# A sixth set of expert weights in a hybrid streaming encoder step on one core

## The reference, cut to what matters

```python
proj = jnp.einsum('blnc,ncd->blnd', branches, w_out)                  # 2 branches x 512 -> 1024
x = x + jnp.sum(gates * proj.astype(jnp.float32), axis=2).astype(x.dtype)
h2 = rmsnorm(x, norm_ffn_g)
x = x + hier_moe(h2, w_router_group, b_router_group, w_router_expert, b_router_expert,
                 w_expert_gate, w_expert_up, w_expert_down)
# in hier_moe, for a block of rows of expert e:
return (jax.nn.silu(xblk @ w_gate[e]) * (xblk @ w_up[e])) @ w_down[e]
```

## Time and profile before

| | |
|---|---|
| median of 3 runs | 1670.44 us (1666.98 to 1670.96) |
| the profiled execution | 1668.39 us |
| its span, first to last instruction | 1666.24 us (shown as 1666.2) |
| mean granted TensorE clock | 0.966 of full speed |
| TensorE busy | 1510.1 us, 91% of the span |
| `merge`, by its first and last instructions | 1113 to 1299 us |
| `experts` | 1300 to the end |

### The profile page before, as it was taken

How to read it: one execution, slowest core, us unless ns; L and a number is a source line. 1 busy time by engine, 2 the same in 40 slices (tenths; PEclk the granted TensorE clock), 3 DMA queues, 4 the chain that set the end, 5 groups by cost and what they waited for, 6 DMA issues and landing times. The chain is left out here.

```text
span 1666.2 us, 38766 instructions
## 1 busy us (share of the span) xinstructions
PE 1510.1 (91%) x16352; PEld 1070.4 (64%) x16352; DVE 861.3 (52%) x1874; ACT 445.3 (27%) x882; POOL 102.2 (6%) x102
## 2 busy tenths in 40 slices
PE   4999999969999999999998699978997799988894
PEld 2888888854566666666667466644554677766663
DVE  2454555455566676767668476645766233211111
ACT  2222222233222333233231244433453111111110
POOL 0000000000000000000000000000000222332321
PEclk9999999989999999999999699999999799999998
DMA  9332221535142232212122444436754699999972
GB/s 323 137 123 88 94 89 63 191 113 181 58 126 68 80 110 68 80 65 71 50 65 59 108 101 100 101 109 255 276 189 154 227 328 349 344 339 323 324 265 36
DMA packets 101326, 259.55 MB, mean 156 GB/s; under 512 B 34240, under 2 KB 53328, under 8 KB 91824
## 3 DMA queue, kind: packets, MB, share of 16 engines
q1 hardware_dynamic: 93424, 239.92, 42.3%
q0 software_dynamic: 7744, 17.33, 4.5%
HBM read 205.32 MB, written 60.56 MB: 160 GB/s over the span
## 5 line engine op out<-in xcount | busy, mean ns | idle before, releaser
L527 PEld LDWEIGHTS a_ps<-a_hT,a_wz 128*128 128x128 f32 x1792 | 202.6, 192 | 3.8 <-issue 3.8
L527 PE MATMUL a_ps<-a_hT,a_wz 128*128 128x128 f32 x1792 | 204.0, 275 | 0.0
L1918 PE MATMUL d_ps<-late,d_oT 128*128 128x512 f32 x256 | 115.4, 598 | 1.5 <-DVE d_oT L1687 0.8
L2089 DVE COPY f_xT<-f_turned 128x384 f32<-128x384 f32 x32 | 17.9, 558 | 164.9 <-PE f_turned L2056 164.9
L1918 PEld LDWEIGHTS d_ps<-late,d_oT 128*128 128x128 f32 x256 | 46.7, 190 | 51.5 <-issue 50.2
L1453 ACT ACTIVATE late<-c_score,c_top 128x1024 f32<-128x1024 f32 (+8 forms) x72 | 50.6, 703 | 93.2 <-DVE c_top L1402 92.6
L1101 PE MATMUL b_ps<-r_wg,r_hT 128*128 128x512 f32 x128 | 64.9, 640 | 11.5 <-POOL b_S L759 9.7
L2283 DVE TENSOR_SCALAR f_y<-f_down,table 96x512 f32<-96x512 f32 x32 | 23.9, 747 | 98.2 <-PE f_down L2082 98.2
L821 DVE TENSOR_TENSOR b_M<-b_ps,r_causal 128x512 f32<-128x512 f32 x72 | 46.4, 686 | 54.5 <-PE b_ps L1162 54.0
L2082 PE MATMUL f_down<-wd,f_midT 128*96 128x512 f32 x160 | 72.8, 598 | 1.8 <-DVE f_midT L2101 1.8
L2290 ACT ACTIVATE f_xT<-f_turned 128x384 f32<-128x384 f32 x32 | 15.7, 491 | 202.7 <-PE f_turned L2056 202.7
(11 more groups left out here) (363 smaller groups left out, 2847.5 us busy)
## 6 DMA issues: line engine op xcount, KB each, us to landing
wgu<-w_gate_up SPq DMA_DIRECT2D x20, 2048.0 KB
late<-w_gate_up SPq DMA_DIRECT2D x12, 2048.0 KB
wd<-w_down SPq DMA_DIRECT2D x20, 1024.0 KB
late<-w_down SPq DMA_DIRECT2D x12, 1024.0 KB
r_hT<-hT_d SPq DMA_DIRECT2D x18, 512.0 KB, 3.9
b_hT<-hT_d SPq DMA_DIRECT2D x18, 512.0 KB, 4.3
gate_d<-b_logits SPq DMA_DIRECT2D x32, 256.0 KB, 2.6
late<-gate_d SPq DMA_DIRECT2D x8, 1024.0 KB, 5.9
```

Source lines behind the costliest of these rows:

```text
L527: mm = pe.matmul(banks[Z_BANKS[n % 2]][:, j * P:(j + 1) * P], wz[:, i, (g + j) * P:(g + j + 1) * P], hT[t % 2][:, i, :], start=(i == 0), s ...
L1918: mm = pe.matmul(banks[2 + u][:], oT[t % 2][:, HB * branch(u) + k, :], wo[:, HB * branch(u) + k, half(u)], start=(k == 0), stop=(k == HB - 1))
L2089: copy(xT[b][:, 4 * half:4 * half + 4, :], turned[half][:, 0:4 * CAP].rearrange("p (a b) -> p a b", b=CAP)).then_inc(s[flag], 1)
```

## The change

The weights get a sixth set. `WB` becomes 6. Gate and up of set 5 (`last_up`, 4096 numbers in each partition) lie in space of their own on the right side of the memory, free once attention is over; they are loaded in `merge` at t = 4. Down of set 5 (`last_down`) lies over the two buffers `oT`, which move there, and is loaded after the last projection. `experts` thus loads 26 sets in its loop, not 27. Three orders are changed beside it: the sample tile's four products are made as one group, four quarters in turn, after both branches are turned; at t = 2, `record(0)` goes ahead of `unit(2, 0)`; and in `experts`, `up` of place 0 goes ahead of `turn` of place 1.

```diff
-WB, WB_EARLY = 5, 3
+WB, WB_EARLY = 6, 3
...
-        oT = [sb(f"oT{j}", [P, 2 * HB, P]) for j in range(2)]
+        oT = keep["oT"]
...
+        LATE = (WB_EARLY, WB_EARLY + 1)
...
                 if 1 <= t <= WB_EARLY:
                     load_up(t - 1)
                     load_down(t - 1)
+                if t == WB_EARLY + 1:
+                    load_up(WB - 1)
...
                 if t == NT - 2:
                     sp.wait_ge(oT_done, NT)
                     sp.wait_ge(x_done, NT - 1)
-                    load_up(WB - 1)
+                    load_up(LATE[1])
             sp.wait_ge(proj_done, units_before(NT))
-            load_up(WB - 2)
-            load_down(WB - 2)
+            load_up(LATE[0])
+            load_down(LATE[0])
+            load_down(WB - 1)
             sp.wait_ge(x_done, NT)
-            load_down(WB - 1)
+            load_down(LATE[1])
...
                 norm(t - 1)
+                if t == 2:
+                    record(0)
                 unit(t, 0)
-                record(t - 2)
+                if t > 2:
+                    record(t - 2)
...
-            def project_tail(b):
+            def project_tail():
+                pe.wait_ge(oT_copied, 2)
                 for k in range(HB):
-                    for u in (b, b + 2):
+                    for u in range(UNITS):
+                        b = branch(u)
...
             turn_branch(0, 1).then_inc(first_ob_done, 1)
-            pe.wait_ge(oT_copied, 1)
-            project_tail(1)
             pe.wait_ge(first_oa_in, 16)
             turn_branch(0, 0).then_inc(oT_done, 1)
-            pe.wait_ge(oT_copied, 2)
-            project_tail(0).then_inc(proj_done, 1)
+            project_tail().then_inc(proj_done, 1)
...
             turn(pe, s, 0, 0, 0)
+            up(pe, s, 0, 0, 0, 0, None)
             turn(pe, s, 1, 1, 0)
-            up(pe, s, 0, 0, 0, 0, None)
...
+            last_up, last_down = (c.enter_context(nc.sbuf_tensor(n, [P, k], F32, side="right")) for n, k in (("last_up", up_size), ("last_down", 2 * D)))
+            keep["wgu"].append(last_up[:].rearrange("p (a b) -> p a b", a=DC))
+            keep["wd"].append(last_down[:].rearrange("p (a b) -> p a b", a=2))
+            keep["oT"] = [last_down[:, D * j:D * (j + 1)].rearrange("p (a b) -> p a b", b=P) for j in range(2)]
```

## The result

The changed kernel takes 1647.69 us (median of 4 runs, 1646.93 to 1648.58) beside 1668.71 us for the kernel before in the same comparison (4 runs, 1666.53 to 1670.96). The ratio is 0.9885, with a 95% interval of 0.987 to 0.99: 19.2 us less. Run again on another chip it gave 0.9906 (0.9886 to 0.9925), 15.7 us less. The forecast was 16.0 us less. Of the 6.7 us, 1.7 are the value that the forecast started from, 1670.44, where this comparison has 1668.71; the median on the other chip is 1650.54. The profiled execution of the changed kernel took 1648.11 us, with a span of 1646.0 us.

A forecast was written before the change was run, and what follows sets the result against it. The last stage was taken as bound by DMA weight loads, with 27.2 us of waits. Terms 9.2 + 3.0 + 0.9 + 0 + 0.9 - 0.2 + 2.2 = 16.0 us took 1670.44 to 1654.4, range 1647.5 to 1662.5.

The forecast's parts named there:

- The starting point: `experts`: DMA brings a set every 11.69 us, TensorE needs 9.68; load backlog, waits 27.2 us, 2 MB alone about 6 us.
- Term 5: Start of `experts`, `up(0)` before `turn` of place 1: first loop load earlier, 0.9 us gained; `last_down` delays first gather 0.2.
- Term 1: `experts` loop loads 26 sets, not 27: 9.2 us gained at 343 GB/s, bounds 7.2 to 11.7; stage stays DMA-bound.
- Term 6: `experts`, gap behind place 26: half of its 4.4 us, 2.2 us gained; bounds 4.4 gained or 3.3 lost.
- Term 2: `merge`, sample tile as one group: four quarters run at once, tile 1 starts 3.0 us earlier; bounds 0.2 to 3.6.
- Term 3: `merge` at t = 2, `record(0)` first: TensorE starts 1.3 us earlier, `router(1)` 0.9 us; bounds 0 and 1.4.
- Term 4: `merge` at t = 4, one more 2 MB load: hidden where the DMA share is 0.18, cost 0.
- The first: Rival, `experts`: TensorE's own "issue" gaps stop hiding in the waits, returning up to 6.7 us, 1661.1 us; chance 0.10.
- The second: Rival, `merge`: load at t = 4 not hidden, gates of tile 6 delay ScalarE, 3 us lost, 1657.4 us; chance 0.04.
- the third: Rival, `experts`: deeper backlog makes instruction blocks late at places 2 to 21, slower, about 1707 us; chance 0.05.
- The fourth: Rival, `experts`: first loop loads, not their number, set the end's pace; Term 1 nothing, about 1663.6 us; chance 0.05.

The follow-up runs named there:

- the change again: The changed kernel run once more, unedited, on another chip beside the kernel before; ratio 0.9906 (0.9886 to 0.9925).
- the kernel of the turn order: Changed kernel with `turn` of place 1 ahead of `up` of place 0 again, as before the change; ratio 0.9896 (0.9865 to 0.9927).
- The pairs: Changed kernel with the sample tile's 32 instructions ordered as quarters 1 and 3, then 0 and 2; group 8.19 us, ratio 0.9902 (0.9876 to 0.9928).
- the kernel of small down loads: Changed kernel with each down load in the loop cut to the first 128 of 1024 columns; 1638.26 us, ratio 0.9829 (0.9811 to 0.9846).
- the seventh buffer: Changed kernel with a seventh gate-and-up buffer over `x`, `junk` and `mixed` of `merge`, down staying at six; 1639.38 us, ratio 0.9827 (0.9809 to 0.9845).

## Why the prediction was right, and where its sizes were off

**The starting point: right, with two figures off.** The backlog is there, but a load of 2 MB alone takes longer than the "about 6 us" of the text: in the profiles that show landings, no gate and up load of `merge` or of the loop lands in less than 8.2 us after its issue. And the hole before the first load of the loop was not empty: the DMA share is 0.56 from 1301 to 1312 in the kernel before. Neither changed the sum: the first gather came no later with `last_down` ahead of it (Term 5).

**Term 1, the set that is no longer loaded in the stage: mechanism right, size too small.** The stage stayed bound by DMA, the places went at 9.68 us until the first wait at place 22, then at (1592.79 - 1501.47) / 8 = 11.4 us, and 14.1 us of waits remained, as forecast (12 to 14). The term had 9.2 us, from 3.146 MB at 343 GB/s, and bounds of 7.2 to 11.7. Measured, the distance from the first load to place 31 fell by 13.3 us on average (12.9 and 14.8 within one order), the stretch until the last landing by 11.7 to 15.8, and the time of the set alone by 14.2. The part that comes from bytes is 10 us and agrees. What the term lacks is that the mean rate of the other 26 sets rose too, by 1 to 2%, which over 300 us is 3 to 6 us. The price of one set was taken as the whole effect, with the rest of the queue unchanged. In size the result is nearer to a whole pace of DMA, 11.69 us, which I had set down as a bound and argued away: "the other traffic goes with the number of experts done and stays". The MB of the rows' queue do stay (14.95 and 14.92), so that sentence holds. The rate was what moved, after the 14th load of the loop, and its cause is open.

**Term 6, the gap behind place 26: wrong.** It gave 2.2 us to an event of one execution. The kernel before without it has the same distance to place 31 within about 1 us. The step that failed is "The DMA pace needed 11.69; the other 4.4 us come from the gap": the other waits were smaller in that execution, and the sum of waits hardly moved (27.2, 26.2, and 25.3 with the orders only). That Terms 1 and 6 together, 11.4, come near to 13.3 is luck: two errors with opposite sign.

**Term 2, the sample tile in one group: right, and it depends on the clock.** Forecast 3.0 of 0.2 to 3.6. Measured 3.4 to 3.55 us in four profiles with the group, the one after and that of the orders alone among them, and 2.3 and 2.2 in two (the change again and the kernel of the turn order), where the clock came back later. The pairs gave 0.5, near the other end. "If four quarters run at once" was decided rightly, from rows that only showed two. The rule of the Trainium skill cited there ("TensorEngine Tiling (Array Packing)", Theoretical Speedup) agrees: at the full clock, 32 instructions in four quarters take the 3.6 us that 16 in two quarters took.

**Term 3, `record(0)` first: right.** `turn_h2(1)` came 1.4 us earlier against tile 1 (29.92 and 31.36), and `router(1)` 0.95, with ScalarE's wait for the gates in between, as forecast. What the term leaves out is the clock: in the one profile of the changed kernel with the old order, the gap of 3.29 us dropped it, and `router(1)` came 3.6 to 3.7 us later than with the change.

**Term 4, the load at t = 4: right.** 0 us there, and 4.6 us at the first gather if it is put at the end.

**Term 5, the first load of the loop: right in its place, without a trace at the end.** It was issued 1.2 us (0.7 in the change again) sooner after the first `turn`. Over nine profiles with the new order the load comes 9.0 to 10.6 us after that `turn` (mean 9.8), over five with the old one 10.5 to 10.8 (mean 10.7), so 0.9 us on average as forecast, and nothing at all in two of the nine. And the gather wasn't later (5.94 and 6.1 us of waiting, 6.2 without the orders). But the kernel with the old order reached place 31 no later. It may be worth 0.9 us at the end; no run here can tell that from nothing.

**The rivals.** The first fell with the kernel of small down loads: no "issue" gap stands where no weights are late. The second fell by the tile times and the third by 150 us of TensorE fully busy from 1320 to 1470 with full DMA. So the refills of which the Trainium skill speaks ("Runtime: NRT & Kernel Launch", Instruction fetch mechanics) held nothing up here. The fourth fell by the ratio of the sixth set alone.

**The sum.** 16.0 us was forecast; the comparisons gave 19.2 and 15.7, and the two profiles shown 20.3. Of these, 2.4 are where `merge` happens to start, 3.55 tile 1, 0.95 `record(0)`, 0.7 the way from there to the first `turn` of `experts`, less 0.5 for the second wait at its start, and 13.2 the places from 2 to 31. So the sum came out near because too little for the set stood beside 2.2 us for a gap that was none and 4.6 us for three orders that gave about 2.3 by themselves. The range given does not follow from the parts named for it either: the fourth rival alone has 1663.6, and the worst ends of all terms have 1667.3. What stays open is why the DMA engines move 323 or 324 GB/s with six sets and 318 to 320 with five; no kernel was run that changes the depth of the queue and leaves the number of loads as it is.

## What to carry to other kernels

If a consumer runs from a store that a slower producer refills, all of the store's depth pays in full as long as waits remain at the end: count the waits left (here 27 us), price one more buffer by its bytes at the stretch's own rate as the least, and take the whole time between two refills as a likely value, not as a far bound. Where the load is put decides whether it is free: the same 2 MB cost nothing in a stretch whose DMA share had been 0.44 (1194 to 1206 in the kernel before) and 4.6 us beside the first gather of the next stage. Take no term from a single event of one execution, and count from a common point in both profiles before subtracting their times.

## What the runs showed of the hardware that was not expected

- The same gap of 3.29 us in front of `turn_h2(1)` left TensorE at 2.4 GHz in the kernel before (twice) and in the one with the sixth set only, and had it at 1.2 GHz in the one with `record(0)` put back, where 16 transposes and 8 products then took 8.6 us in sum and not 5.7. The instructions ahead of the gap are of the same kinds in all of them.
- The same 32 products of the sample tile took 5.15 us and 6.49 us in two executions of one kernel, with a mean granted clock of 0.70 and 0.55 over them.
- An issue of a weight load in `experts`, mostly 0.3 to 0.8 us, took up to 5.06 us with six sets (at 1535.75), and five more between 1490 and 1560 took over 2 us. It was up to 6.51 us in the other profiles with six sets and 7.58 with the seventh buffer, and never over 1 us with five. The chain that ended last holds no issue of more than 1 us in the profiles with six sets that were followed back (the one after, the change again, the sixth set only).
- The traffic of the rows, gathers and adds together, weighs more than its bytes: the rows' queue moved 14.95 MB in 20.2% of the engines' time, 234 GB/s, and the weights 84.87 MB in 73.6%, 365 GB/s.
